# Queries of tokens 256 to 511 moved from ahead of the second tile's retrieval to beside it, in a fused attention, convolution and expert-retrieval block

## What is computed

```
proj = h @ w_in;  attn = ... @ w_attn_o;  conv = ... @ w_conv_o
y = (g_attn * attn + g_conv * conv) @ w_out          # "out"
x = x + gate1 * rms_norm(y, g[1]);  h = rms_norm(x, g[2]) * (1.0 + scale2) + shift2
q = (h @ w_q).reshape(B, S, PEER_HEADS, 2, PEER_HALF)       # "queries"
s1 = einsum('bshc,hnc->bshn', q[..., 0, :], sub_keys[:, 0])  # "scores", s2 likewise
v1, i1 = top_k(s1, 16);  v2, i2 = top_k(s2, 16)
top, ci = top_k(v1[..., :, None] + v2[..., None, :], 16)     # per head, 8 heads
expert = ea * 128 + eb;  gate = softmax(top)
pre = einsum('td,tkd->tk', h, expert_down[expert])           # 128 rows of 2048 per token
act = gelu(pre) * gate;  out = einsum('tk,tkd->td', act, expert_up[expert])
```

## Time and profile before

| | us |
|---|---|
| median of three runs | 4179.17 (4174.87 to 4181.80) |
| the profiled execution | 4181.56 |
| its span | 4178.9 |
| PE busy | 2812.1 (67%) |
| DVE busy | 2278.5 (55%) |
| POOL busy | 1387.0 (33%) |
| ACT busy | 541.3 (13%) |

### The profile page before, as it was taken

How to read it: one execution, slowest core, us unless ns; L and a number is a source line. 1 busy time by engine, 2 the same in 40 slices (tenths; PEclk the granted TensorE clock), 3 DMA queues, 4 the chain that set the end, 5 groups by cost and what they waited for, 6 DMA issues and landing times.

```text
span 4178.9 us, 37663 instructions
## 1 busy us (share of the span) xinstructions
PE 2812.1 (67%) x15140; PEld 1595.7 (38%) x15140; DVE 2278.5 (55%) x3525; ACT 541.3 (13%) x1191; POOL 1387.0 (33%) x1109
## 2 busy tenths in 40 slices
PE   5999899899899999997973434434444444434435
PEld 3787788798755554553540100101101100101101
DVE  6399779642643333325664565664656664444442
ACT  3211221201200101012120100100100110000000
POOL 2321211010022333322334454534434444344342
PEclk9999999999899999998985555555555555555556
DMA  9353332898467898986879999999999999999998
GB/s 365 141 231 111 152 137 105 310 414 314 182 234 307 354 380 337 357 331 241 339 288 421 388 406 421 421 422 421 421 421 418 421 422 419 418 422 421 421 421 371
DMA packets 201837, 1413.23 MB, mean 338 GB/s; under 512 B 24384, under 2 KB 24512, under 8 KB 31936
## 3 DMA queue, kind: packets, MB, share of 16 engines
q0 software_dynamic: 152064, 1107.36, 64.6%
q1 hardware_dynamic: 43680, 291.53, 18.4%
q10 hardware_dynamic: 5920, 11.94, 0.8%
HBM read 1403.35 MB, written 7.39 MB: 338 GB/s over the span
## 4 chain that ended last, share of the span: by engine, by line
PE 41%; DMA 39%; DVE 11%; POOL 4%; issue 3%; ACT 2%; ACTq 0%; DVEq 0%; SPq 0%; POOLq 0%
PE psum L605 41%; DMA front<-in_down,back 30%; DMA front<-in_up,back 6%; DVE front L1604 4%; POOL front L576 3%; DVE back L1372 2%; DVE back L1341 1%; DMA front<-in_w_conv_o 1%; ACT back L1134 1%; POOL x_low L560 1%; DMA back<-in_x 1%; DVE back L1705 0%; ACT front L1238 0%; DVE back L1595 0%; DMA back<-in_up,back 0%
## 5 line engine op out<-in xcount | busy, mean ns | idle before, releaser
L605 PE MATMUL psum<-front 128*32 128x512 f32 (+2 forms) x6608 | 1393.9, 661 | 914.2 <-DMA front<-in_up,back 854.0
L1604 DVE CUSTOM_DVE_ANT_0 front<-front,back 128x2048 f32<-128x2048 f32 x512 | 1170.8, 2292 | 1372.7 <-DMA front<-in_down,back 1240.6
L605 PEld LDWEIGHTS psum<-front 128*32 128x32 f32 (+1 forms) x6608 | 566.7, 160 | 1676.4 <-issue 1422.9
L576 POOL DMA_INDIRECT front<-in_down,back x512 | 595.7, 1163 | 909.2 <-DVE back L1604 671.5
L605 PE MATMUL psum<-back,front 128*32 128x128 f32 (+3 forms) x4400 | 645.1, 462 | 333.3 <-DMA back<-in_up,back 173.0
L576 POOL DMA_INDIRECT front<-in_up,back x442 | 511.2, 1157 | 1020.3 <-PE psum L605 968.5
L605 PEld LDWEIGHTS psum<-back,front 128*32 128x32 f32 (+1 forms) x4400 | 376.5, 169 | 608.7 <-issue 343.5
L554 POOL TENSOR_TENSOR w_low<-front,w_high 128x2048 fp32r<-128x2048 f32 x33 | 155.2, 4702 | 539.1 <-ACT w_high L1022 539.1
L605 PE MATMUL psum<-x_high,w_high 128*128 128x512 f32 x640 | 252.3, 394 | 9.4 <-POOL x_low L560 6.6
L605 PE MATMUL psum<-x_low,w_high 128*128 128x512 f32 x640 | 251.0, 392 | 0.0
L605 PE MATMUL psum<-x_high,w_low 128*128 128x512 f32 x640 | 250.7, 392 | 0.0
(11 more groups left out here) (161 smaller groups left out, 1677.0 us busy)
## 6 DMA issues: line engine op xcount, KB each, us to landing
front<-in_w_in SPq DMA_DIRECT2D x116, 1024.0 KB, 7.0
back<-in_ada_w SPq DMA_DIRECT2D x64, 1024.0 KB, 7.8
front<-in_ada_rows POOLq DMA_DIRECT2D x32, 1024.0 KB, 13.6
front<-in_w_out SPq DMA_DIRECT2D x32, 1024.0 KB, 5.8
front<-in_w_q SPq DMA_DIRECT2D x32, 1024.0 KB, 5.1
front<-in_w_conv_o SPq DMA_DIRECT2D x16, 1024.0 KB, 8.6
front<-in_w_attn_o SPq DMA_DIRECT2D x16, 512.0 KB, 11.3
front<-in_down,back POOLq DMA_INDIRECT x512, 20.4
```

The lines of the kernel that those rows point to most:

```text
L576: nc.gpsimd.indirect_dma_start(out=row_, out_offset=None, in_=table[:, :], in_offset=bass.IndirectOffsetOnAxis(ap=idx4[:, t % 2, c:c + 1], ...
L605: return nc.tensor.matmul(o, a, b, start=start, stop=stop)
L1604: V.tensor_tensor_reduce(d_row[s], d_row[s], h2r, 1.0, 0.0, ALU.mult, ALU.add, pre[:, b // 16 % 2, b % 16:b % 16 + 1]).then_inc(dots_done, 1)
```

## The change

`tail(1)` no longer makes the queries and scores of its 384 tokens in one pass. A first pass ("q", "sc") makes those of tokens 128 to 255 (tile 1), a second ("q2", "sc2") those of tokens 256 to 511 (tiles 2 and 3). Both load all 16 chunks of w_q; `tail(1)` has 99 chunks.

`PACE` is now weighted: the first 83 chunks share 128 blocks by a work of 12 for a chunk of ga, gc, co and out, 6 for ao, 9 for x and 4 for q (about 1.9, 0.95, 1.4 and 0.63 blocks), and the last 16 (q2) get 128 + 7 (i + 1) // 4, that is 1.75 blocks each, up to position 156. The position after the last "out" chunk is 114 (before 98), and 21 instead of 18 after the first column group.

The scores of a group are issued before the retrieval that follows its last chunk, not after it. ACT does the last exponent of tile 1's gates (`gate_exp(c, 3)`) ahead of the second pass. DVE's first routing step of tile 2, at block 156, now also waits for the last copy of sc2. The gathers of block 160 wait for the new end of the tail. `tail_groups` is one list for all counts; `tail(0)` is as before but for the place of its scores.

```diff
+QUERIES = ((("", 0, P),), (("", P, P), ("2", 2 * P, 2 * P)))
+
+
+def tail_groups(c):
+
+    out = [(kind, cg, k) for cg in range(4) for kind, k in (("ga", 4), ("gc", 4), ("ao", 2), ("co", 2))]
+    out += [("out", i, 4) for i in range(4)] + [("x", t, 1) for t in range(TAIL[c][1] // P)]
+    for go, _, _ in QUERIES[c]:
+        out += [(kind + go, i, k) for i in range(4) for kind, k in (("q", 4), ("sc", 0))]
+    return out
...
 def tail_chunks(c):
-    return 4 * 12 + 16 + TAIL[c][1] // P + 16
+    return sum(k for _, _, k in tail_groups(c))
+
+
+TAIL_END = DONE[1, "sc2", 3] + 4
 
 
 def block_pace():
 
-    return [(i + 1) * 128 // tail_chunks(1) for i in range(tail_chunks(1))]
+
+    work = [k * (12 if kind in ("ga", "gc", "co", "out") else 6 if kind == "ao" else 9 if kind == "x" else 4) / max(k, 1)
+            for kind, _, k in tail_groups(1) for _ in range(k)][:-16]
+    out = [round(128 * at / sum(work)) for at in itertools.accumulate(work)]
+    return out + [128 + 7 * (i + 1) // 4 for i in range(16)]
...
-                for i in range(4):
-                    for s in range(4):
-                        rows(w_q, i, s)
-                        behind(c)
+                for _ in QUERIES[c]:
+                    for i in range(4):
+                        for s in range(4):
+                            rows(w_q, i, s)
+                            behind(c)
...
                     if i == WIDE:
-                        pool.wait_ge(g_done, DONE[1, "sc", 3] + 4)
+                        pool.wait_ge(g_done, TAIL_END)
...
+                        if s == chunks - 1 and behind is not None:
+                            behind()
                         chunk_out(c)
...
+                for go, q0, qn in QUERIES[c]:
+                    for i in range(4):
+                        def scores():
+                            for m in range(4):
+                                pe.wait_ge(act_took, ATOOK[c, "q" + go, i] + m + 1)
+                                for t in range(qn // P):
+                                    ins = mm(ps[:, m, t * P:(t + 1) * P], sqt[:, m, t * P:(t + 1) * P], keys[c][:, 4 * i + m, :], True, True)
+                                ins.then_inc(g_done, 1)
+                        tq = slice(q0, q0 + qn)
+                        if i:
+                            group(4, 4, hT, plain, act_took, ATOOK[c, "sc" + go, i - 1], None, tq, scores)
...
+                        passed(c, 1)
+                        if not go and i:
+                            gate_exp(c, i - 1)
+                    if c and not go:
+                        gate_exp(c, 3)
...
                     if n == 0 and t >= 2:
                         dve.wait_ge(u_used, 128 * (t - 1))
+                        dve.wait_ge(act_took, ATOOK[1, "sc2", 3] + 4)
...
                 gates(c, 3)
+                if c:
+                    for _ in range(4):
+                        passed(c, 4)
```

More of the change, by code:

```diff
@@ L81, in tail_counts @@
     d = a = v = 0
[L82 to L86, removed]
+    for c in range(len(TAIL)):
+        for kind, i, _ in tail_groups(c):
             done[c, kind, i], act[c, kind, i], dve[c, kind, i] = d, a, v
@@ L102, in chunk_ends @@
     out, plain = [], 0
[L103 to L106, removed]
+    for c in range(len(TAIL)):
+        for kind, i, k in tail_groups(c):
             for _ in range(k - 1):
@@ L109, in chunk_ends @@
                 out.append((False, plain))
-            out.append((True, DONE[c, kind, i] + 4))
+            if k:
+                out.append((True, DONE[c, kind, i] + 4))
     return out
@@ L895, in tail, with group @@
                 tok = slice(t0, t0 + n)
-                def group(chunks, per, src, place, free, base, between=None):
+                def group(chunks, per, src, place, free, base, between=None, tok=tok, behind=None):
+                    n = tok.stop - tok.start
                     for s in range(chunks):
@@ L978, in tail @@
                 pe.wait_ge(keys_in, 16 * (c + 1))
[L979 to L988, removed]
+                for go, q0, qn in QUERIES[c]:
[9 more added lines that the diff above has]
+                            group(4, 4, hT, plain, act_took, ATOOK[c, "sc" + go, i - 1], None, tq, scores)
+                        elif go:
+                            group(4, 4, hT, plain, act_took, ATOOK[c, "sc", 3], None, tq, scores)
+                        else:
+                            group(4, 4, hT, plain, dve_took, VTOOK[c, "x", n // P - 1], None, tq, scores)
             tail(0)
@@ L1238, in tail @@
                     A(hT[:, k, tok], hT[:, k, tok], ACT.Identity, scale=modc[:, 2, k:k + 1], bias=modc[:, 1, k:k + 1]).then_inc(h2_ready, 1)
[L1239 to L1253, removed]
+                for go, q0, qn in QUERIES[c]:
+                    for i in range(4):
+                        passed(c, 3)
+                        for m in range(4):
+                            act.wait_ge(g_done, DONE[c, "q" + go, i] + m + 1)
+                            if m == 0 and i:
+                                act.wait_ge(g_done, DONE[c, "sc" + go, i - 1] + 4)
+                            elif m == 0 and go:
+                                act.wait_ge(g_done, DONE[c, "sc", 3] + 4)
+                            A(sqt[:, m, 0:qn], ps[:, m, 0:qn], ACT.Copy).then_inc(act_took, 1)
+                        for m in range(4):
+                            act.wait_ge(g_done, DONE[c, "sc" + go, i] + m + 1)
+                            for t in range(q0 // P, (q0 + qn) // P):
+                                ins = A(sc[t][:, 4 * i + m, :], ps[:, m, t * P - q0:(t + 1) * P - q0], ACT.Copy)
+                            ins.then_inc(act_took, 1)
+                        passed(c, 1)
[3 more added lines that the diff above has]
+                        gate_exp(c, 3)
                 if c == 0:
@@ L1259, in _ @@
             tail(1)
-            gate_exp(1, 3)
             retrieve(END)
```

## The result

The changed kernel takes 4121.99 us in the median of four runs (4120.09 to 4125.06), against 4179.35 for the kernel before: a ratio of 0.986, with a 95% interval of 0.9848 to 0.9872. It is faster by 57 us, where the forecast was 35. The profiled execution has a span of 4120.9 us, 58.0 less than before.

A forecast was written before the change was run, and what follows sets the result against it. Span taken as bytes at 421 GB/s plus time when DMA is not full, PE limiting two stretches before block 160. 14 + 8 + 9 - 106 + 30 + 10 = -35 us from 4179 gives 4144 us; range 4106 to 4190.

The forecast's parts named there:

- Part 3: Queries and routing of tile 1, first query chunk to block 128: DVE becomes the bound, 106 us gained.
- Part 2: First column group: DVE does 16 dots instead of 13 before taking PE's "ao" result, PE waits; +9 us, bounds 0 and 13.
- part 1: Blocks pulled forward, up to the last "out" chunk: 14 us more PE, plus 8 us for waits (bounds 0 and 42).
- Part 4: Third load of w_q: twelve loads fall into blocks 128 to 156, where DMA is full; +30 us, PE's work hidden.
- Part 5: Friction in blocks 128 to 156: waits for ACT's copies and sc2, PE's clock; +10 us, bounds 0 and 50.
- The rule against it: Skill's rule that matmul batches shorter than the DMA wait behind them start slow; would put the second pass at half clock.
- the rival of 4249 us: Half clock: PE at 1.2 GHz throughout the second pass, 105 us more; chance 0.04.
- No cover in the first stretch: Rival: mixed traffic in stage 1 gets 360 GB/s, 33 us more than counted, 4177 us; chance 0.13.
- Lockstep: Rival: a stop of PE, ACT or DVE at a group's end stops POOL; part 5 is 60, 4204 us; chance 0.09.
- The good case: Rival, all cover holds: parts 1, 2 and 5 at 0 but for the 14; 4117 us, chance 0.14.

The follow-up runs named there:

- The run with shorter routings: Changed kernel without the second routing step of tile 1 (places 9 to 16 of the 16 best scores): 4112.96 us, ratio 0.9846.
- The run of the passes alone: Changed kernel with the old even table for its first 83 chunks (1.54 blocks each), second pass as it is: 4189.26 us, ratio 1.0025 to the kernel before.
- The runs with the slower start: Changed kernel with the old pace in the first column group, two blocks per chunk in the second: 4123.34 us; with routings 3 and 4 late too: 4105.9 us.
- the run with small loads: Changed kernel, the 16 second-pass loads of w_q fetching only 32 of 512 columns each: 4104.36 us, ratio 0.982.
- two routings late: Changed kernel with tile 1's third and fourth routings moved behind blocks 128 to 139: 4103.52 us, ratio 0.9816.
- more matmuls: Changed kernel with 5 matmuls for 4 in the second pass of queries: 4128.87 us; with 8 for 4: 4201.9 us.
- late routings: Changed kernel with tile 1's last routing moved behind block 128: 4119.42 us; with the third moved as well: 4103.52 us.

## Why the prediction was right, and where its sizes were off

**What bounds the kernel.** Right. Behind block 160 both kernels run at one pace, and the gain of the stretch before it came out at the end but for 2 us. The size was off by 22 us: 4122 lies inside the range but outside the band from 4125 to 4167 that had most of the chance.

**Part 3, -106.** Measured -107.4, and by the mechanism named: DVE's routings in a row, 24.5 to 27.7 us apart, eight dots between them, and DVE never idle for more than 0.8 us. The run with shorter routings shows DVE as the bound. That is no luck; each of its terms can be found in the timeline. What the step did not see is how much it rests on the table: it took DMA's and PE's rhythm in that stretch one by one and found both shorter than DVE's. The run of the passes alone shows that together they can be worse than each by itself, 210 us where the bytes explain 169.

**Parts 1 and 2, +31.** Measured +17.0. Part 2's 9 us came as forecast: DVE's product ended at 1249.4 instead of 1240.5, and PE went on 8.9 us later. From there to the first query chunk it was 8.2 us more, where part 1 had 14 + 8:

```profile
1239.25:1952.29 713.04, 666.09 (x2829) 357.56 (x2829) 267.75 (x301) 83.77 (x197) 213.19 (x172) 0.97 0.85 336
```

```profile
1248.10:1969.30 721.20, 678.15 (x2949) 359.02 (x2949) 295.07 (x326) 92.32 (x217) 264.17 (x200) 0.97 0.92 372
```

The first row is of the kernel before, the second of the changed one. PE is busy 12 us more, close to the 14. But its other time fell by 4 us instead of growing by 8: it never waited for a gathered row from 1264 to 1965, and a wait for DVE in the fourth column group went from 4.75 us to 1.37. The term that failed is the 8 us for waits on full DMA. (Its bytes were counted as 216 + 30 MB, where 16 blocks of 2.1 MB are 34; the window from 1264 to 1908 moved 245.) The runs with the slower start do not show that part 2's wait was covered, for the reason given there.

**Parts 4 and 5, +40.** Measured +30.7. Part 4 was right: exactly twelve full loads fell between blocks 128 and 160, and SP's transfers took 30.5 us more of DMA there than before. Part 5, 10 us of friction, is the other term that failed: DMA was idle 3 us in that stretch, no more than before, and what the run with small loads leaves for it is 5 us at most.

The forecast's 35 is thus the measured 60 at block 160 less 25: 14 in the first stretch, 9 in the second pass, 1 in part 3. The terms priced from instructions and bytes (14, 9, -106, 30) came within 2 us each; the two set for waits that no row showed (8 and 10) did not come, and 4 us of old waits went away.

**The rule against it.** Slow starts did occur. The last three quarters of the turning at block 128, behind a wait of 21.8 us, took 1.48, 1.48 and 1.25 us; before, 1.48, 1.48 and 0.81 behind 11.5. Of the 15 chunks behind it three took 7.5 to 8.1 us instead of 6.8, each behind one of the longer waits (3.2 to 3.5 us on PEld). That is 3 us in all: the granted clock from 2088.3 to 2247 is 0.97. PE waited for rows 11 times between 2093 and 2290:

```profile
PE psum L621 <- DMA front<-in_up,back: 26.8, 11, 3.9
```

The Trainium skill (TensorE: Matmul & The Clock Gate, "HAM oscillation — how this bites in real kernels") says of matmul batches that are shorter than the DMA wait behind them that each of them starts slow. The prediction carried it over to the second pass without that condition. Here the batches, 7 us and longer, were longer than their waits, 3.9 us at most, so this kernel does not test the rule as the page has it; the rival of 4249 us, PE at 1.2 GHz throughout, did not come.

**The other rivals.** No cover in the first stretch: it ran at 381 GB/s, near the 387 that the forecast took as proof, so cover held. Lockstep: at most 5 us, not 60. The good case, 4117 us, is what came: its terms are 14, -106 and 30, measured were +17.0, -107.4 and +30.7, and the result is 5 us above it, 22 below the forecast. That its first term fits so well is in part luck: it put part 2's wait at nothing, which came in full, while part 1 was 8 us and not 14. It had a chance of 0.14, too low beside the 0.60 of a forecast whose two terms for waits stood on no row.

## What to carry to other kernels

Work that must be done, but not yet, can be moved from a stretch that an engine bounds to one that DMA bounds even at the price of loading its weights again, if the engine's time fits beside the bytes there: here 16.8 MB bought 107 us for 31, and the table that made it possible cost 17. Such a move is only as good as the pacing around it: one in-order queue that serves two consumers (here POOL, with `down` rows for DVE and `up` rows for PE) stops both when either is busy elsewhere, and a table of order has to be made anew with the move. In a sum of costs, those priced from instructions and bytes held here; those set for waits that no row showed did not. And a load made small in bytes may keep its packets: look up what it still costs in DMA's time before the rest is called waiting.

## What the runs showed of the hardware

The DMA engines, with gathers of 8 KB rows and loads of 1 MB side by side, reached 402 to 410 GB/s where all engines had work in flight (402 over 197 us and 410 over 159 us in the changed kernel, 405 over 91 us with two routings late), close to the 421 of gathers alone.

Small packets cost DMA more than their bytes: with small third loads, 6528 packets and 1.05 MB from SP took 5.9 us of the 16 engines, where 1920 packets and 12.85 MB took 31.2.

One kernel does not start a stretch at one time: the first query chunk began between 1961.1 and 1974.5 us in six kernels that are the same up to there (the runs with shorter routing, small third loads, more matmuls and late routings), and 5 us of that stand already at PE's restart in the first column group (1244.5 to 1249.4). A difference of a few microseconds at one place of two traces is therefore no finding by itself.
